# Block 2's two attention stages interleaved with weight chunks, for both layers

## The reference, cut to what matters

```
x = layer_norm(A*x + 0.5*swiglu(x))                 # ffn 1
z = x @ w_in          # queries, keys, values of three branches, gates, forget logits
o_a = nsa(...)        # 8 heads: compressed (15 keys) + selected + window attention, gated sum
o_b = swa_sink(...)   # 8 heads: band attention with a sink and a relative bias
o_c = fox(...)        # 8 heads: causal attention, bias c_q - c_k, c = cumsum(log_sigmoid(f + b_f))
g = sigmoid(x @ w_gate + b_gate)                    # three gates of 1024 columns
mix = (g_a*(o_a @ w_a) + g_b*(o_b @ w_b) + g_c*(o_c @ w_c)) @ w_out
x = layer_norm(A*x + mix)
x = layer_norm(A*x + 0.5*swiglu(x))                 # ffn 2
```

## Time and profile before

| | us |
|---|---|
| median of 3 runs | 2724.89 (2720.43 to 2728.8) |
| the profiled execution's own time | 2719.38 |
| its span, first to last instruction | 2717.6 |
| PE busy | 2499.9 (92% of the span) |
| DVE busy, ACT busy | 1528.3 (56%), 1274.4 (47%) |
| mean granted clock of PE | 0.941 |

### The profile page before, as it was taken

How to read it: one execution, slowest core, us unless ns; L and a number is a source line. 1 busy time by engine, 2 the same in 40 slices (tenths; PEclk the granted TensorE clock), 3 DMA queues, 4 the chain that set the end, 5 groups by cost and what they waited for, 6 DMA issues and landing times. The chain is left out here.

```text
span 2717.6 us, 46615 instructions
## 1 busy us (share of the span) xinstructions
PE 2499.9 (92%) x17862; PEld 2264.9 (83%) x17862; DVE 1528.3 (56%) x2679; ACT 1274.4 (47%) x1972; POOL 232.2 (9%) x228
## 2 busy tenths in 40 slices
PE   6898789999889799999989999999999989898998
PEld 4776468887778589999886889899899868798998
DVE  4489663334558655655455555554554564655554
ACT  6364652232546554434455454533533554545433
POOL 0023000000013000022000000121121000000220
PEclk9898899999999899999995999999999967899999
DMA  8321022222533035554440334445345422153552
GB/s 315 132 102 61 1 94 95 93 107 93 201 140 109 14 132 180 176 195 178 148 179 28 119 125 172 147 179 185 145 180 184 146 88 109 71 181 138 181 182 101
DMA packets 59959, 367.16 MB, mean 135 GB/s; under 512 B 5872, under 2 KB 17184, under 8 KB 17312
## 3 DMA queue, kind: packets, MB, share of 16 engines
q1 hardware_dynamic: 59664, 365.05, 37.0%
q10 hardware_dynamic: 144, 0.01, 0.0%
HBM read 357.66 MB, written 7.37 MB: 134 GB/s over the span
## 5 line engine op out<-in xcount | busy, mean ns | idle before, releaser
L210 DVE TENSOR_TENSOR w_lo<-ring,w_hi 128x1024 fp32r<-128x1024 f32 x652 | 820.4, 1300 | 533.3 <-ACT w_hi L198 533.2
L252 PE MATMUL psum<-x_hi,w_hi 128*128 128x256 f32 (+1 forms) x3392 | 1037.8, 306 | 62.9 <-DVE x_lo L605 21.9
L253 PE MATMUL psum<-x_lo,w_hi 128*128 128x256 f32 (+1 forms) x3392 | 1029.6, 304 | 0.0
L254 PE MATMUL psum<-x_hi,w_lo 128*128 128x256 f32 (+1 forms) x3392 | 1029.3, 303 | 0.0
L198 ACT ACTIVATE w_hi<-ring 128x1024 fp32r<-128x1024 f32 (+1 forms) x652 | 653.3, 1050 | 341.7 <-PE psum L254 156.3
L252 PEld LDWEIGHTS psum<-x_hi,w_hi 128*128 128x128 f32 x3392 | 657.3, 194 | 95.1 <-issue 59.4
L253 PEld LDWEIGHTS psum<-x_lo,w_hi 128*128 128x128 f32 x3392 | 657.4, 194 | 24.8 <-issue 1.9
L254 PEld LDWEIGHTS psum<-x_hi,w_lo 128*128 128x128 f32 x3392 | 657.0, 194 | 23.3
L1604 PE MATMUL psum<-h_hi,w_hi 128*128 (+1 forms) x640 | 181.1, 283 | 0.0
L1606 PE MATMUL psum<-h_lo,w_hi 128*128 (+1 forms) x640 | 181.1, 283 | 0.0
L1607 PE MATMUL psum<-h_hi,w_lo 128*128 (+1 forms) x640 | 181.1, 283 | 0.0
(11 more groups left out here) (278 smaller groups left out, 3153.8 us busy)
## 6 DMA issues: line engine op xcount, KB each, us to landing
ring<-wstream SPq DMA_DIRECT2D x327, 1024.0 KB, 4.8
kept_hi<-x_hi SPq DMA_DIRECT2D x1, 2048.0 KB, 6.3
kept_lo<-x_lo SPq DMA_DIRECT2D x1, 2048.0 KB, 12.7
x_hi<-kept_hi SPq DMA_DIRECT2D x1, 2048.0 KB, 7.9
x_lo<-kept_lo SPq DMA_DIRECT2D x1, 2048.0 KB, 12.3
rel_bias<-bias_by_distance SPq DMA_DIRECT2D x2, 1024.0 KB, 7.5
na_bias<-rpb SPq DMA_DIRECT2D x4, 438.0 KB, 5.8
cst<-consts SPq DMA_DIRECT2D x1, 1662.0 KB, 11.7
```

Source lines behind the costliest of these rows:

```text
L210: dve.tensor_tensor(w_lo[:, c % 2, h], ring[:, (c + 2 * i) % RING, h], w_hi[:, c % 2, h].bitcast(F32), ALU.subtract).then_inc(split_done.s ...
L252: pe.matmul(o, w_hi[:, c, w_cols], hi, start=first, stop=False)
L253: pe.matmul(o, w_hi[:, c, w_cols], lo, start=False, stop=False)
L254: return pe.matmul(o, w_lo[:, c, w_cols], hi, start=False, stop=last)
```

## The change

For both layers of block 2, A and B become one stage, and C and D become one stage.

`woven` writes out one list of items for all engines: the steps of an attention, and between them half chunks, spread evenly. In the first stage (`attend_and_project`) the 24 steps and their 4 steps of drain lie among the 18 half chunks of the projection; `Forget` is cut into nine parts, one behind every second step. In the second (`attend_and_merge`) the 16 + 4 steps lie among the first 26 half chunks of the merge; the other 18 follow without steps. On ACT a half chunk means: take the chunk before out of PSUM (at a first half), then round half of the next chunk; on DVE: the remainder of that half, then the take.

With PSUM shared by chunks and attention, scores have one set of banks where there were three and transposes one bank; PE's step t now waits for `biased` of t-1 before its scores, and for the copy of the transposes before. The output of a pair is no longer copied and split again: ACT writes its rounded part and DVE the remainder directly to where the queries were (`halves`). The sigmoid becomes Tanh of half the argument, (tanh + 1)/2, with the factor 1/2 given back when y is split. Block 1 keeps its stages; its `Attention` only has renamed helpers.

```diff
 
-            def __init__(self, steps, dst, bufs):
+            def __init__(self, steps, dst, bufs, turn_bank=None, outs=(3072, 3584), halves=False):
                 self.steps, self.dst, self.U = steps, dst, len(steps)
+                self.turn_bank, self.outs, self.halves = turn_bank, outs, halves
...
-            def bank(self, u, half, a, n):
-                at = ((u % self.SETS) * 2 + half) * 512 + a
+            def score(self, u, half, n):
+                at = 512 * half + (1024 if self.turn_bank else 1024 * (u % self.SETS))
                 return psum[:, at:at + n]
 
+            def turn(self, u, half, a):
+                at = self.turn_bank + 256 * half if self.turn_bank else 1024 * (u % self.SETS) + 512 * half
+                return psum[:, at + a:at + a + P]
+
             def out(self, pair):
-                at = 3072 + (pair % 2) * 512
-                return psum[:, at:at + 512]
+                at = self.outs[pair % 2]
+                return psum[:, at:at + (256 if self.halves else 512)]
...
                     u = self.steps[t]
-                    if t >= self.SETS:
+                    if self.turn_bank and t:
+                        pe.wait_ge(biased.sem, self.base[biased] + 2 * t)
+                    elif t >= self.SETS:
                         pe.wait_ge(turned_sb.sem, self.at(turned_sb, t - self.SETS))
...
                     pe.wait_ge(scaled.sem, self.at(scaled, v))
+                    if self.turn_bank and v:
+                        pe.wait_ge(turned_sb.sem, self.at(turned_sb, v - 1))
                     for half in range(2):
                         for a, w in self.blocks(v):
-                            mm = pe.transpose(self.bank(v, half, a, P)[0:w],
+                            mm = pe.transpose(self.turn(v, half, a)[0:w],
                                               self.prob[:, v % self.PROBS, half, a:a + w], const("ident"))
...
-                v = t - self.LAG_V
-                if v in self.ends:
+                v = t - self.LAG_V - int(self.halves)
+                if v in self.ends and self.halves:
+                    pair = self.steps[v]["pair"]
+                    hi, lo = self.dst(pair)
+                    dve.wait_ge(taken_hi.sem, self.at(taken_hi, pair))
+                    dve.tensor_tensor(lo, self.out(pair)[:, 0:lo.shape[1]], hi.bitcast(F32), ALU.subtract
+                                      ).then_inc(taken.sem, 1)
+                elif v in self.ends:
...
+                v = t - self.LAG_V
+                if self.halves and v in self.ends:
+                    pair = self.steps[v]["pair"]
+                    hi, _lo = self.dst(pair)
+                    act.wait_ge(summed.sem, self.at(summed, v))
+                    act.activation(hi, self.out(pair)[:, 0:hi.shape[1]], ACT.Copy).then_inc(taken_hi.sem, 1)
...
+                    qc = [sb("qc", [P, 4, S], F32R, stack=st, side="right") for _ in range(2)]
+                    kkb = [sb("kkb", [P, 2, S], F32R, stack=st, side="right") for _ in range(2)]
+                    fox_bias = [sb("fox_bias", [P, HEADS, P * (qt + 1)], stack=st, side="right") for qt in range(2)]
+                    forget = Forget(layer, v_b, fox_bias, st)
+                    bufs = attention_buffers(st, S, side="right")
+                    near = Attention(nsa_steps(qa, kkc, kks, kkw, v_sw, vc, gates), in_place_of(qa), bufs,
+                                     turn_bank=3072, outs=(512, 2560), halves=True)
+                    attend_and_project(near, forget, [
+                        *queries(qb), ("kk", (kkb[0][:], kkb[1][:]), 1.0), *queries(qc),
+                        ("kk", (kkf[0][:, 0:2, :], kkf[1][:, 0:2, :]), 1.0),
+                        ("kk", (kkf[0][:, 2:4, :], kkf[1][:, 2:4, :]), 1.0),
+                        ("r", v_c[:, 0:4:2, :], 1.0), ("r", v_c[:, 1:4:2, :], 1.0)])
                 with ExitStack() as st2:
                     y = sb("y", [P, KT, S], stack=st2)
                     sg = sb("sg", [P, 4, S], stack=st2)
...
+                    others = Attention(other_steps(layer, (qb, qc), kkb, kkf, v_b, v_c, fox_bias),
+                                       lambda pair: in_place_of((qb, qc)[pair // 4])(pair % 4), bufs,
+                                       turn_bank=3072, outs=(2560, 3584), halves=True)
+                    attend_and_merge(others, (qa, qb, qc), y, sg, prod, par(layer, "half_b_gate"),
+                                     Moments(list(range(KT)), 1024))
...
+        def woven(steps, halves, extra=()):
+            out, done = [], 0
+            for t in range(steps):
+                out.append(("step", t, 0))
+                out += [("extra", e, 0) for e, after in extra if after == t]
+                while done * steps < halves * (t + 1):
+                    out.append(("half", done // 2, done % 2))
+                    done += 1
+            return out
...
+        def round_ahead(act, j, half):
+            c = g0[0] + j + 1
+            if half == 0:
+                act.wait_ge(landed[c % 2].sem, 16 * (c // 2 + 1))
+                act.wait_ge(chunk_done.sem, c - 1)
+            round_half(act, c, 0, half)
+        def attend_and_project(a, forget, plan):
...
+            items = woven(a.length, 2 * n, [(e, 2 * e + 1) for e in range(forget.PARTS)])
...
+                    for what, j, half in items:
+                        if what == "step":
+                            a.pe(pe, j)
+                        elif what == "extra":
+                            forget.pe(pe, j)
+                        else:
+                            kind, o, _ = plan[j]
+                            if kind == "r":
+                                mm = pe_half_rows(pe, j, half, o.shape[2])
+                            else:
+                                mm = pe_half_columns(pe, j, half, hi, lo, KT, lambda m: acc(j, S, S * m))
+                            if half:
+                                mm.then_inc(chunk_done.sem, 1)
+
...
+                    def take(j):
+                        kind, o, scale = plan[j]
+                        act.wait_ge(chunk_done.sem, g0[0] + j + 1)
+                        act.wait_ge(acc_free.sem, g0[0] + j)
+                        if kind == "r":
+                            act.activation(o, result(j)[:, :, 0:o.shape[2]], ACT.Copy).then_inc(acc_free.sem, 1)
+                        else:
+                            act.activation(o[0], result(j), ACT.Copy, scale=scale).then_inc(upper.sem, 1)
+
+                    for what, j, half in items:
+                        if what == "step":
+                            a.act(act, j)
+                        elif what == "extra":
+                            forget.act(act, j)
+                        else:
+                            if j and half == 0:
+                                take(j - 1)
+                            round_ahead(act, j, half)
+                    take(n - 1)
...
+                    def take(j):
+                        kind, o, scale = plan[j]
+                        if kind == "kk":
+                            dve.wait_ge(upper.sem, u0 + halves.index(j) + 1)
+                            dve.scalar_tensor_tensor(out=o[1], in0=result(j), scalar=scale, in1=o[0].bitcast(F32),
+                                                     op0=ALU.mult, op1=ALU.subtract).then_inc(acc_free.sem, 1)
+
+                    for what, j, half in items:
+                        if what == "step":
+                            a.dve(dve, j)
+                        elif what == "extra":
+                            forget.dve(dve, j)
+                        else:
+                            rest_half(dve, g0[0] + j + 1, 0, half)
+                            if j and half == 0:
+                                take(j - 1)
+                    take(n - 1)
...
+        def attend_and_merge(a, branches, y, sg, prod, bias, moments):
...
+            spread = 2 * seq.index(("proj", 2, 0)) - 2
+            items = woven(a.length, spread)
+            items += [("half", j, h) for j in range(n) for h in range(2) if 2 * j + h >= spread]
...
+                            def operand_made(k):
+                                if b:
+                                    pe.wait_ge(taken.sem, k0 + 4 * (b - 1) + k + 1)
+                            mm = pe_half_columns(pe, j, half, lambda k: branches[b][0][:, k, :],
+                                                 lambda k: branches[b][1][:, k, :], 4,
+                                                 lambda m: projected(j, m // 2)[:, m % 2 * S:m % 2 * S + S],
+                                                 operand_made)
...
+                        if kind == "merge":
+                            act.wait_ge(chunk_done.sem, g0[0] + j + 1)
+                            act.wait_ge(acc_free.sem, g0[0] + j)
+                            for m in range(2):
+                                at = 8 * b + 2 * i + m
```

(47 more changed lines are left out.)

332 lines of the change are left out of this document (206 added, 126 removed).

## The result

The changed kernel takes 2687.98 us in the median (2685.28 to 2690.66, 4 runs), the kernel before, measured beside it, 2722.66 (2720.13 to 2728.8, 4 runs): a ratio of 0.9869, 95% interval 0.9848 to 0.9891. The change makes it faster by 1.3%, 35 us. Some 20 us of them belong to the two woven stages; most of the rest goes with a shift of the buffers that the change brings along (experiment 1). The forecast was 2667 (2640 to 2702): the direction is right and the time is in the range, but 21 us above the forecast.

What follows compares the result with a forecast made beforehand. The prediction took a chain through DVE and ACT as the bound. Gains of 24.3 and 4.6 made 28.9 per layer, 57.8 for both, so 2719.4 became 2661.6, or 2667 against the median; range 2640 to 2702.

Steps and rivals of the forecast that it cites:

- This is what I think decides: Both woven stages: waits between DVE and ACT in program order set the time, 97 and 105 us.
- chain through DVE and ACT: Maximum, exponentials, rounding and remainder wait in turn; first woven stage: 3.9 us a turn with a half chunk, 1.5 without.
- PE's 93.8: First woven stage, PE's work alone: 32 attention, 51.8 chunks, 7.6 `Forget`, 2.4 mostly first chunk at low clock.
- PE's 99.1: Second woven stage to the last step, PE's work alone: 24.2 for 16 steps, 74.9 for 26 half chunks.
- 161: Whole second woven stage: 105 with steps, then 51.8, 3.3 and 1; a gain of 4.6 from 165.7.
- rival 1: Both woven stages: PE sets the pace, 38 gained per layer, 2643, or 2649 against the median; chance 0.23.
- 2 for PE results that it waits for: First woven stage, `Forget`: ACT's waits for PE results, 2 us within the 97.
- the bias additions: First woven stage, `Forget`: 16 additions on DVE, 5.4 us, cost nothing while ACT exponentiates and rounds.
- Rival 2: First woven stage: clock drops at 8 steps without a half chunk, +15 per layer, 2697; chance 0.15.
- Rivals 3 and 4: Clock low through the whole first woven stage, 2796, chance 0.05; Tanh and Exp not sharing a table, 2718, chance 0.05.

Runs made afterwards that it cites:

- experiment 1: The kernel before with only the changed kernel's 24 more columns in `vec`, unused: 2713.27 us against 2733.9 for the kernel before, ratio 0.9928.
- Experiment 4: The changed kernel with one stage's list written unwoven: 2709.89 us without the first weaving, 2699.33 us without the second.
- experiment 5: The changed kernel with PE's forget parts one step later in its list, DVE's and ACT's left in place: 2665.6 us.
- 9: On top of experiment 5, the second stage's steps spread over 20 half chunks instead of 26: 2667.43 us.
- experiment 8: On top of experiment 5, PE's half chunks in quarters, and ACT and DVE taking the half chunk before the step: 2680.41 us.
- 7: On top of experiment 5, ACT and DVE take the half chunk before the step in the first stage: 2663.95 us.

## Why the prediction was right, and where it was not

**Right.** A's matmuls gained the full clock for most of the stage, C's gaps were filled, the kernel got faster with its time inside the range. That it lies there owes something to luck: the first woven stage was missed by 20 us per layer, and the layout, which I had not priced, gave part of that back. Waits of PE's scores for DVE are few (2.3), as argued. Tanh shares the table. Experiment 4 shows that both weavings carry gain: 21.9 and 11.4.

**The step that failed: "This is what I think decides".** I set the first woven stage by a chain through DVE and ACT, at 97, a little over PE's 93.8. It took 117.2, and the chain did not set it: DVE and ACT are about half idle, and moving only PE's forget parts (5) takes 10.4 per layer out. My chain added its terms up in every turn. In most turns they run beside PE's half chunk instead, since ACT and DVE prepare a half ahead, and PE waits only 3.5 us (2.3 + 1.2) before scores and transposes. PE's own floor of 93.8 was too low as well: the steps take 33.9 and not 32, a half chunk 3.07 and not 2.88. Without the waits for `Forget` (5) the stage still takes 106.8. In the second woven stage I said 105 to the last step against PE's 99.1. There PE has no gap, and in 9 a spread for which my chain asks 10 us or more costs nothing. From 1550.6 to the norm's first matmul at 1707.0 it is 156.4, where I had 161 and rival 1 155.2. **Rival 1 (PE sets the pace) holds there,** with 8.6 gained in layer 0 where I gave it 10.5 and my own forecast 4.6. The chain exists, but only experiment 8 made it close.

**The term that was missing: the wait for `Forget`.** I gave "2 for PE results that it waits for" and counted the bias additions as hidden behind ACT. I asked who hides the additions and not who waits for them: PE's part waits at the same place of the lists for what DVE does there after everything else, and the next half chunk is queued behind it. It cost 7.7 per layer in waits; with it gone (5), 10.4 per layer are gone. The diff shows it: `bank` returns one bank where there were four, beside the wait on `mixed` in PE's part. I had asked of the banks of the scores what was queued behind; the same question belonged here.

**Rival 2 (the clock drops) held in part.** I had it at the eight steps without a half chunk, at 15 per layer. The mean of 0.92 over 117.2 is some 19 us at 0.50: the first 5.7 are the start that I had counted, and four stretches of 3.4 us follow, from 1445.9, 1459.6, 1473.2 and 1486.9. The last of them and the rest of the stage:

```profile
1486.90:1490.30 3.40, 3.07 (x7) 2.53 (x8) 0.18 (x1) 0.00 (x0) 0.00 (x0) 0.50 0.57 234
1490.30:1550.60 60.30, 53.85 (x454) 45.18 (x452) 35.88 (x132) 29.94 (x81) 0.00 (x0) 1.00 0.20 71
```

Each of the four begins within 5 us of the start of one of the first four steps without a half chunk, and near a wait of PE (0.64 until 1444.4, 1.10 until 1457.2, 0.85 until 1472.6, 2.57 until 1487.2). Behind 1490.3 stand the other four such steps, and the clock is 1.00. So a step without a half chunk alone does not lower it, and neither does each wait: 2.08 until 1498.9 and 2.21 until 1508.7 left it at 1.00. In 5, with the waits for `Forget` gone, the last two of the four stretches are gone as well, while the steps there are the same. So fewer waits went with fewer drops; which wait makes one stays open.

**Rivals 3 and 4 fell:** the clock is 0.92, not 0.50; there is no table load between gates.

**Not foreseen:** the feed-forward, 8.5 of the 30 us between the spans, by 24 columns that I had not priced, and up to 4.5 more in the mixing (1).

**The sum again.** First woven stage 20.2 over the forecast, second 4.6 under: 15.6 per layer, 31.2 if both layers are taken like layer 0; the feed-forward 8.5 under and block 1's 5.5 over leave 28.2 over 2661.6, or 2689.8. The profiled execution's own time is 2689.6, of which 1.8 lie outside its span of 2687.8. Without the Forget wait (5) the median is 2665.6. That this meets my 2667 is in part chance: the parts of it are not mine.

## What to carry to other kernels

When the lists of several engines are woven, go through each wait of the engine that is to be the bound and ask where its releaser stands in the other list: a producer and a consumer put at the same place with one buffer between them stop each other, and one place of distance was worth about 21 us of mixing here, for two changed lines of code. Two reorderings that do no harm alone can close a loop together (experiment 8), so the combination is measured, never added. And before a gain is put down to an edit, the kernel before should run with the changed layout alone.

## What the runs showed of the hardware

- **Buffer addresses change PE's pace.** At clock 1.00 and busy throughout, 1502 or 1531 matmuls stand in 180 us, by a shift of 192 bytes of the buffers behind `vec`; shifts of 64 and 128 bytes gave nearly nothing (the four feed-forward stretches sum to 734.1 and 735.8, against 735.2 without a shift and 724.0 with 192 bytes). The rule is open.
- **The clock falls in a dense stage too.** Between dense half chunks it fell to 0.50 near waits of 0.64 to 2.57 us, and not at two others of 2.08 and 2.21; at 0.50 a dense matmul takes 0.213 instead of 0.12. The same wait can go either way: in every kernel here with the second stage changed, PE waits 2.0 for the operand of the `out` chunks. Behind it the clock fell in layer 0 of experiment 5 and stayed in that of 7, where this part of the code is the same:

```profile
1670.00:1690.00 20.00, 18.35 (x140) 18.35 (x141) 10.38 (x12) 7.82 (x9) 0.00 (x0) 0.91 0.39 141
```

```profile
1670.00:1690.00 20.00, 18.01 (x150) 17.80 (x149) 11.44 (x14) 8.65 (x10) 0.00 (x0) 1.00 0.47 177
```

The Trainium skill ("TensorE: Matmul & The Clock Gate", section "Part 1: The HAM clock gate") ties the clock to how busy PE has been. The rows agree in part: in the windows from 1460 to 1490 the granted clock is 0.84 in the changed kernel, where PE is busy for 26.49 us, and 0.98 in experiment 5, where it is busy for 28.98; but A stayed at 0.50 with PE busy for 56.09 of 58.50 us.
- **Attention alone comes at either clock.** The same kernel before kept the low clock in C until 1567 in one execution and until 1604 in another; layer 0's mixing differs by 11.4 us between the two. With weight chunks between the steps the changed kernel's four runs lie within 5.4 us.
